# Another order of the expert blocks in a mixture-of-experts step: wide blocks in twos at three places, the fullest expert between two small blocks, two small blocks last

## The reference

```python
logits = x2 @ w_router + b_router             # 536 tokens, 32 experts
top_v, top_i = lax.top_k(logits, 4)
gates = jax.nn.softmax(top_v, axis=-1)
# for each expert e, on the tokens xe that chose it:
gu = xe @ w_gate_up[e] + b_gate_up[e]         # 1024 -> 2048
gate, up = gu[:, :1024], gu[:, 1024:]
gate = jnp.minimum(gate, 7.0)
up = jnp.clip(up, -7.0, 7.0)
h = gate * jax.nn.sigmoid(1.702 * gate) * (up + 1.0)
yb = h @ w_down[e] + b_down[e]                # 1024 -> 1024
# y[token] = sum over its 4 experts of gates * yb
```

## Time and profile before

| | |
|---|---|
| median of 3 runs | 1348.79 us (1348.22 to 1349.29) |
| profiled execution | 1349.23 us |
| its span, first to last instruction | 1347.4 us |
| TensorE busy | 1248.3 us, 93% of the span |
| VectorE busy | 831.6 us, 62% |
| ScalarE busy | 608.9 us, 45% |
| moved by DMA | 457.16 MB, mean 339 GB/s |
| of that on SyncE's queue | 435.28 MB, 78.9% of 16 engines' span |

### The profile page before, as it was taken

One profiled execution on the slowest core, in us unless ns is written; L12 is line 12 of the kernel. 1 busy time (PEld: TensorE's weight loads), 2 busy tenths in 40 slices (PEclk: granted clock), 3 DMA queues, 4 the chain that ended last, 5 costly groups with the idle time before them and its releaser, 6 DMA issues.

```text
span 1347.4 us, 18886 instructions
## 1 busy us (share of the span) xinstructions
PE 1248.3 (93%) x6184; PEld 807.3 (60%) x6185; DVE 831.6 (62%) x1352; ACT 608.9 (45%) x826; POOL 145.8 (11%) x158
## 2 busy tenths in 40 slices
PE   7999999899999999999999999799999999999992
PEld 5888854477574747464656576264747474656550
DVE  3896668699393837464655596182937464655643
ACT  4111342478273545354444574172735354453632
POOL 8100011010001010101101000100010101101000
PEclk9999999989999999999999999999999999999996
DMA  9610176399999999999999984999999999999984
GB/s 322 87 38 1 52 259 287 131 334 411 355 417 412 419 411 419 405 422 405 414 409 400 416 364 180 406 419 406 421 408 421 404 412 397 401 417 388 421 341 139
DMA packets 67333, 457.16 MB, mean 339 GB/s; under 512 B 15916, under 2 KB 19508, under 8 KB 34520
## 3 DMA queue, kind: packets, MB, share of 16 engines
q1 hardware_dynamic: 56344, 435.28, 78.9%
q0 software_dynamic: 10944, 21.30, 6.7%
HBM read 440.26 MB, written 23.50 MB: 344 GB/s over the span
## 4 chain that ended last, share of the span: by engine, by line
PE 42%; DMA 20%; DVE 8%; issue 5%; ACT 4%; DVEq 0%; SPq 0%; ACTq 0%; POOLq 0%; POOL 0%
PE bank L2144 24%; DMA ring_lo<-in_w_gate_up 15%; PE bank L2254 12%; DVE w_lo L2376 6%; DMA ymix<-ffn_in,idx_next 3%; ACT w_hi L1964 3%; PE bank L2265 2%; DMA token_sums<-ymix,row_cur 1%; PE bank L2134 1%; PE bank L2127 1%; DVE cmix L2394 1%; DVE cmix L2397 1%; PE bank L2230 1%; ACT cmix L1983 0%; PE bank L2274 0%
## 5 line engine op out<-in xcount | busy, mean ns | idle before, releaser
L2376 DVE TENSOR_TENSOR w_lo<-ring_lo,w_hi 128x1024 fp32r<-128x1024 f32 x271 | 315.6, 1220 | 101.0 <-ACT w_hi L1964 99.9
L1964 ACT ACTIVATE w_hi<-ring_lo 128x1024 fp32r<-128x1024 f32 x271 | 270.2, 1052 | 86.8 <-DMA ring_lo<-in_w_gate_up 64.4
L2254 PE MATMUL bank<-ring_lo,x_s 128*64 128x512 f32 x960 | 215.9, 597 | 0.4 <-ACT x_s L1973 0.4
L2144 PE MATMUL bank<-w_hi,x_hi 128*128 128x512 f32 x544 | 179.5, 412 | 8.9 <-DVE x_lo L2382 6.7
L2144 PE MATMUL bank<-w_lo,x_hi 128*128 128x512 f32 x544 | 173.8, 402 | 0.0
L2144 PE MATMUL bank<-w_hi,x_lo 128*128 128x512 f32 x544 | 172.2, 398 | 0.0
L2376 DVE TENSOR_TENSOR w_lo<-w_out,w_hi 128x1024 fp32r<-128x1024 f32 x136 | 161.7, 1220 | 6.0 <-ACT w_hi L1964 5.2
L1964 ACT ACTIVATE w_hi<-w_out 128x1024 fp32r<-128x1024 f32 x136 | 140.0, 1053 | 31.8 <-PE bank L2144 31.6
L1892 POOL DMA_INDIRECT token_sums<-ymix,row_cur x33 | 57.2, 1732 | 742.3 <-ACT ymix L1994 705.3
L2254 PEld LDWEIGHTS bank<-ring_lo,x_s 128*64 128x64 f32 x960 | 65.0, 137 | 119.1 <-issue 117.0
L2144 PEld LDWEIGHTS bank<-w_hi,x_hi 128*128 128x128 f32 x544 | 102.4, 196 | 40.1 <-issue 18.8
(11 more groups left out here) (444 smaller groups left out, 1407.4 us busy)
## 6 DMA issues: line engine op xcount, KB each, us to landing
ring_lo<-in_w_gate_up SPq DMA_DIRECT2D x128, 2048.0 KB, 18.8
w_out<-in_w_down SPq DMA_DIRECT2D x128, 1024.0 KB, 20.5
ring_lo<-in_w_in SPq DMA_DIRECT2D x3, 2048.0 KB, 21.1
w_out<-in_w_out SPq DMA_DIRECT2D x2, 2048.0 KB, 8.7
x<-in_x_prompt SPq DMA_DIRECT2D x6, 512.0 KB, 11.3
bias<-bias_rows SPq DMA_DIRECT2D x132, 3.0 KB
ring_lo<-in_w_in SPq DMA_DIRECT2D x2, 1024.0 KB, 9.7
token_sums<-x SPq DMA_DIRECT2D x4, 512.0 KB
```

What stands on the lines that cost most here:

```text
L1964: nc.scalar.activation(high(j), raw(j), ACT.Copy).then_inc(s["w_hi"], 1)
L2144: last = nc.tensor.matmul(bank[b + u][:], v[:, k, :], part(j)[:, u, :], start=(j == 16 and first), stop=(k == KD - 1 and part is high and ...
L2254: last = nc.tensor.matmul(bank[2 * half][64 * u:64 * u + 64, :], x_s[:, k % 4, 64 * (k // 4):64 * (k // 4) + 64], gu[:, k, :, half, 256 * ...
L2376: v.tensor_tensor(low(j), raw(j), high(j).bitcast(F32), ALU.subtract).then_inc(s["w_lo"], 1)
```

## The change

The core of the diff (the same order is written out on ScalarE and VectorE as well; the line numbers of the changed file are other ones):

```diff
@@ -47,12 +47,19 @@
 GATE_MAX = LIMIT / (1.0 + math.exp(-ALPHA * LIMIT))
 S_SLOTS = P // 2
 Q_SLOTS = P // 4
-EARLY, LATE = 7, 7
-TOP = 2 * EARLY + 2
+PAIRS = (3, 3, 3, 3)
+FIRST_EXTRA = 2 + 2 * PAIRS[0]
+TOP = FIRST_EXTRA + 2 + 2 * PAIRS[1]
 REST_OF_TOP = TOP + 1
-FINAL = TOP + 2 * LATE + 2
+SECOND_EXTRA = TOP + 2 + 2 * PAIRS[2]
+FINAL = SECOND_EXTRA + 2 + 2 * PAIRS[3]
 NPOS = FINAL + 1
-SMALL_RANK = EARLY + LATE + 3
+SMALL_RANK = sum(PAIRS) + 5
+RUNS = (2, FIRST_EXTRA + 1, TOP + 2, SECOND_EXTRA + 1)
+SMALLS = (0, PAIRS[0], PAIRS[0] + PAIRS[1] + 2, PAIRS[0] + PAIRS[1] + PAIRS[2] + 2)
+WIDES = (2, PAIRS[0] + 3, PAIRS[0] + PAIRS[1] + 4, PAIRS[0] + PAIRS[1] + PAIRS[2] + 5)
+TOP_WIDE, TOP_SMALL = WIDES[2] - 1, SMALLS[2] - 1
+LAST_SMALL = sum(PAIRS) + 3
...
+            g.iota(pairs[:, 0], pattern=[[1, n]], base=SMALL_RANK + SMALLS[run] - run // 2, channel_multiplier=0)
+            g.iota(pairs[:, 1], pattern=[[1, n]], base=WIDES[run] + 1 - run // 2, channel_multiplier=0)
...
+        def pair_loads(run, i, extra=False):
+            q = RUNS[run] + 2 * i
+            load_behind_small(expert_at(sp, q + 1), q + 1, i + SMALLS[run])
+            load_behind_wide(expert_at(sp, q + 2), q + 2, i + WIDES[run], not extra)
+
+        with sp.Fori(0, PAIRS[0] - 1) as i:
+            pair_loads(0, i)
+        pair_loads(0, PAIRS[0] - 1, True)
+        load_behind_wide(expert_at(sp, FIRST_EXTRA + 1), FIRST_EXTRA + 1, WIDES[1] - 1, True)
+        with sp.Fori(0, PAIRS[1]) as i:
+            pair_loads(1, i)
+        load_behind_small(expert_at(sp, TOP), TOP, TOP_SMALL - 1)
         bias_rows_small(expert_at(sp, REST_OF_TOP), REST_OF_TOP)
-        load_behind_small(expert_at(sp, TOP + 2), TOP + 2, EARLY, True)
-        with sp.Fori(0, LATE) as i:
-            load_behind_small(expert_at(sp, 2 * i + (TOP + 3)), 2 * i + (TOP + 3), i + (EARLY + 1))
-            load_behind_wide(expert_at(sp, 2 * i + (TOP + 4)), 2 * i + (TOP + 4), i + (EARLY + 3), True)
+        load_behind_small(expert_at(sp, TOP + 2), TOP + 2, TOP_SMALL, True)
+        with sp.Fori(0, PAIRS[2] - 1) as i:
+            pair_loads(2, i)
+        pair_loads(2, PAIRS[2] - 1, True)
+        load_behind_wide(expert_at(sp, SECOND_EXTRA + 1), SECOND_EXTRA + 1, WIDES[3] - 1, True)
+        with sp.Fori(0, PAIRS[3]) as i:
+            pair_loads(3, i)
+        load_behind_small(expert_at(sp, FINAL), FINAL, LAST_SMALL - 1, True)
...
+        def pair(run, i, side, extra=False):
+            q = RUNS[run] + 2 * i
+            gather(q + 1)
+            added(q - 1)
+            scatter(q, side, 2)
+            gather(q + 2, 1 if extra else 2)
+            added(q)
+            scatter(q + 1, 1 - side)
+
+        with pool.Fori(0, PAIRS[0] - 1) as i:
+            pair(0, i, 0)
+        pair(0, PAIRS[0] - 1, 0, True)
+        gather(FIRST_EXTRA + 1, 2)
+        added(FIRST_EXTRA - 1)
+        scatter(FIRST_EXTRA, 0)
+        with pool.Fori(0, PAIRS[1]) as i:
+            pair(1, i, 1)
         gather(TOP)
         added(TOP - 2)
-        scatter(TOP - 1, 1)
...
+            pair(3, i, 1)
+        gather(FINAL, 2)
+        added(FINAL - 2)
+        scatter(FINAL - 1, 1, 2)
...
-        def small(q, side, sq, loads, lq=None):
+        def small(q, side, sq, loads, lq=None, next_parts=4):
             for half in range(2):
                 if half == 0:
                     act.wait_ge(t["s_first"], t0["s_first"] + sq + 1)
@@ -2055,10 +2087,13 @@
                 take_x(q + 1)
                 split(loads + 1, lq, 2)
                 split(loads + 1, lq, 3)
+            elif next_parts == 2:
+                take_x_small(q + 1)
             act.wait_ge(t["s_used"], t0["s_used"] + LOADS * sq + LOADS)
             take_y(q, side, [4], [512])
             if lq is None:
-                take_x_quarter(q + 1)
+                if next_parts == 4:
+                    take_x_quarter(q + 1)
...
-                if k == 4 and next_parts == 1:
+                if k == 4 and next_parts < 4:
                     pe.wait_ge(s["idx"], q + 2)
-                    x_transposes(q + 1, 1)
-                    set_bias(q + 1)
+                    x_transposes(q + 1, next_parts)
+                    if next_parts == 1:
+                        set_bias(q + 1)
+                    else:
+                        set_bias_small(q + 1)
                 small_down(k)
...
-        small(FINAL, EARLY + LATE + 1, FINAL, over_expert(pe, 0), 4)
+
+        def pair(run, i, extra=False):
+            q = RUNS[run] + 2 * i
+            small(q, i + SMALLS[run], q + 1 if run < 2 else q, expert_at(pe, q + 1), 1)
+            wide(q + 1, i + WIDES[run], expert_at(pe, q + 2), 1 if extra else 2)
+
+        with pe.Fori(0, PAIRS[0] - 1) as i:
+            pair(0, i)
+        pair(0, PAIRS[0] - 1, True)
+        wide(FIRST_EXTRA, WIDES[1] - 1, expert_at(pe, FIRST_EXTRA + 1), 2)
+        with pe.Fori(0, PAIRS[1]) as i:
+            pair(1, i)
+        small(TOP - 1, TOP_SMALL - 1, TOP, expert_at(pe, TOP), 1)
+        wide_with_rest(TOP, TOP_WIDE, TOP_SMALL, expert_at(pe, REST_OF_TOP), expert_at(pe, TOP + 2))
+        with pe.Fori(0, PAIRS[2] - 1) as i:
+            pair(2, i)
+        pair(2, PAIRS[2] - 1, True)
+        wide(SECOND_EXTRA, WIDES[3] - 1, expert_at(pe, SECOND_EXTRA + 1), 2)
+        with pe.Fori(0, PAIRS[3]) as i:
+            pair(3, i)
+        small(FINAL - 1, LAST_SMALL - 1, FINAL - 1, expert_at(pe, FINAL), 2)
+        small(FINAL, LAST_SMALL, FINAL, over_expert(pe, 0), 4)
         overflow(pe, over)
 
     @block.vector
...
+        def small_to_small(q, side, sq, e_next):
+
+            pick(e_next, zero[:, 0:1], 2)
+            next_slots(q, side, 2, sq + 1)
+            small_swiglu(q, 0)
+            small_swiglu(q, 1)
```

More of the change, by code:

```diff
@@ L1919, in _ @@
         scatter(1, 1)
[L1920 to L1929, removed]
+        def pair(run, i, side, extra=False):
[14 more added lines that the diff above has]
+            pair(1, i, 1)
         gather(TOP)
         added(TOP - 2)
-        scatter(TOP - 1, 1)
+        scatter(TOP - 1, 1, 2)
         gather(REST_OF_TOP, 4)
@@ L1938, in _ @@
         scatter(REST_OF_TOP, 1, 4)
-        with pool.Fori(0, LATE) as i:
-            gather(2 * i + (TOP + 3))
-            added(2 * i + (TOP + 1))
-            scatter(2 * i + (TOP + 2), 0, 2)
-            gather(2 * i + (TOP + 4), 2)
-            added(2 * i + (TOP + 2))
-            scatter(2 * i + (TOP + 3), 1)
+        with pool.Fori(0, PAIRS[2] - 1) as i:
+            pair(2, i, 0)
+        pair(2, PAIRS[2] - 1, 0, True)
+        gather(SECOND_EXTRA + 1, 2)
+        added(SECOND_EXTRA - 1)
+        scatter(SECOND_EXTRA, 0)
+        with pool.Fori(0, PAIRS[3]) as i:
+            pair(3, i, 1)
+        gather(FINAL, 2)
+        added(FINAL - 2)
+        scatter(FINAL - 1, 1, 2)
         added(FINAL - 1)
@@ L2082, in _, with pair @@
         wide(1, 1, 1, 2, 2)
-        with act.Fori(0, EARLY - 1) as i:
-            small(2 * i + 2, 0, i, 2 * i + 3, i + 2)
-            wide(2 * i + 3, 1, i + 2, 2, 2 * i + 4)
-        small(TOP - 2, 0, EARLY - 1, TOP - 1, EARLY + 1)
-        wide(TOP - 1, 1, EARLY + 1, 1, TOP)
-        wide_with_rest(TOP, 0, EARLY + 2, EARLY, TOP + 1)
-        with act.Fori(0, LATE) as i:
-            small(2 * i + (TOP + 2), 0, i + (EARLY + 1), 2 * i + (TOP + 2), i + (EARLY + 3))
-            wide(2 * i + (TOP + 3), 1, i + (EARLY + 3), 2, 2 * i + (TOP + 3))
-        small(FINAL, 0, EARLY + LATE + 1, FINAL)
-        overflow(act, lambda b: quarter(b + NPOS, b + (EARLY + LATE + 2)))
+        def pair(run, i, side, extra=False):
+            q = RUNS[run] + 2 * i
+            loads = q + 1 if run < 2 else q
+            small(q, side, i + SMALLS[run], loads, i + WIDES[run])
+            wide(q + 1, 1 - side, i + WIDES[run], 1 if extra else 2, loads + 1)
+        with act.Fori(0, PAIRS[0] - 1) as i:
+            pair(0, i, 0)
+        pair(0, PAIRS[0] - 1, 0, True)
+        wide(FIRST_EXTRA, 0, WIDES[1] - 1, 2, FIRST_EXTRA + 1)
+        with act.Fori(0, PAIRS[1]) as i:
+            pair(1, i, 1)
+        small(TOP - 1, 1, TOP_SMALL - 1, TOP, TOP_WIDE)
+        wide_with_rest(TOP, 0, TOP_WIDE, TOP_SMALL, TOP + 1)
+        with act.Fori(0, PAIRS[2] - 1) as i:
+            pair(2, i, 0)
+        pair(2, PAIRS[2] - 1, 0, True)
+        wide(SECOND_EXTRA, 0, WIDES[3] - 1, 2, SECOND_EXTRA)
+        with act.Fori(0, PAIRS[3]) as i:
+            pair(3, i, 1)
+        small(FINAL - 1, 1, LAST_SMALL - 1, FINAL - 1, next_parts=2)
+        small(FINAL, 0, LAST_SMALL, FINAL)
+        overflow(act, lambda b: quarter(b + NPOS, b + (LAST_SMALL + 1)))
         def square(q):
```

67 lines of the change are left out of this document (33 added, 34 removed).

## The result

The changed kernel takes 1341.66 us (median of 4 runs, 1340.89 to 1341.85), the kernel before 1349.04 us beside it (4 runs, 1348.22 to 1349.68): a ratio of 0.9947, interval [0.9934, 0.9959]. The prediction said 1341.7. A second comparison gave 1341.09 against 1347.62 us, 0.9952 [0.9939, 0.9966]. The profiled execution took 1341.48 us, with a span of 1339.6 and a mean clock of 0.976.

A forecast was written before the change was run, and what follows sets the result against it. The weight stream was taken to pace the blocks of experts. Gains of 3.1 us (hole) and 4.0 us (end), 7.1 us off the profiled 1349.23, gave 1342.1; allowing for its 0.44 us above the median, 1341.7 us, range 1337 to 1348.5.

The forecast's parts named there:

- in every pair of the first half: Pairs of a small and a wide block: the chain of waits goes through the wide block's fourth weight load.
- The twos of wides cost nothing: Adjacent wide blocks at positions 7/8 and 23/24: costed at nothing, at most 4.4 us each.
- The backlog: Weight loads queued ahead in the steady pairs: about 12 us of other work, hiding the 4.4 us of a second wide block.
- 9 positions of 32.5 us: From position 7's fourth load landing at 508.96 us to position 16's, expected at 801.4 us.
- a sign of being wrong: Behind one of the twos of wides: a DMA share clearly under 1 would show the prediction wrong.
- The hole, 3.1 us: Empty queue at the overflow: its products begin at 822.1 instead of 825.24 us, ending it 3.1 us sooner; bounds 0 and 6.
- The end, 4.0 us: Last small block, behind another small one, is paced by its loads and ends at 1316.0 us: 4.0 us gained, bounds 0 and 6.
- the turn through the other engines: Last small block: 1 us added for the turn through ScalarE and VectorE, which has less to hide behind.
- The lower clock: Last block: TensorE's clock at 1.2 GHz after a wait of some 2 us could cost 1 to 2 us.
- A: Only one of the two gains, at the overflow or the last block, comes: some 1345 us; chance 0.13.
- B: Nothing changes: empty stretch at the overflow and end as long as before, or gains given back; 1348.8 us, chance 0.14.
- C: Late gathers of the second wide blocks at both twos drain the queue: slower, some 1354.5 us; chance 0.11.

The follow-up runs named there:

- the early gather: Changed kernel with the gather of position 19 ahead of the wait for the fullest expert's scatter: 1342.96 us, 0.9965 of the kernel before.
- the first half alone: Kernel before with only the first-half order changed (wides at 7 and 8, fullest expert behind a small block), run twice: ratios 0.9993 and 0.9981 to it.
- each half: Kernel before with only the first-half or only the second-half order changed, each run twice: ratios 0.9993 and 0.9981, then 0.9974 and 0.9973.
- Five wides: Changed kernel with five wide blocks in a row at positions 7 to 11 and four small ones at 12 to 15: 1345.37 us, 0.998 of before.
- the best kernel: Changed kernel with the overflow's products ahead of unit 14 of the fullest expert and the gather of position 19 earlier: 1337.64 and 1337.27 us.

## Why the prediction was right, point by point

**What bounds it.** The stream of weights, and at the overflow TensorE as well. (In the first pair, positions 2 and 3, the chain before had no weight load yet; the prediction's "in every pair of the first half" holds from the second pair on.) To give TensorE time (the early gather, a third small block last) brought nothing; to let the loads go out sooner brought 3.5 us, but only once TensorE could follow. The second condition was not in the prediction, which took an earlier load behind the overflow as a gain by itself; at the 2.5 us of this change it did hold (the first half alone, with the load 2.8 to 3.0 us earlier, kept 2.0 to 2.3 us of it).

**The twos of wides cost nothing.** Nearly. The backlog covers one step of 4.4 us with some 8 to spare: at position 8 the first product follows the last one of position 7 with no gap (536.4 us), and the share is 1.01 in the stretch around it. But the step "9 positions of 32.5 us" from the fourth load of position 7 to that of position 16 came out 1 us long: 800.9 − 507.6 = 293.3 us, and 293.6 in the second profile, against the 292.5 of the sum. From the fourth load of position 23 to that of position 32 it was 1301.92 − 1010.71 = 291.2 us, and 291.0 in the second profile, against 9 × 32.2 = 289.8. Behind the second two the share is a little under 1, which the prediction named as a sign of being wrong; but the kernel before has as low a share behind a single wide block. The changed kernel first, then the kernel before:

```profile
1040.00:1080.00 40.00, 39.51 (x190) 29.14 (x190) 28.70 (x37) 23.81 (x28) 5.38 (x4) 1.00 0.95 378
```

```profile
1080.00:1120.00 40.00, 37.72 (x173) 24.76 (x173) 22.03 (x31) 17.84 (x22) 3.82 (x3) 0.96 0.96 393
```

So where the 1 us and the 1.2 to 1.4 us went, and whether the twos cost them, is not shown.

**The hole, 3.1 us.** Right in its mechanism, 0.6 us too large: 552.9 − 550.45 = 2.45 us. The 20.7 us from the fourth load to the overflow's products were right (821.36 − 800.86 = 20.5); the landing of that load was the part that was off: 800.86 − 273.04 = 527.8 us after the first product, where the sum had 801.4 − 274.4 = 527.0.

**The end, 4.0 us.** The whole of 6.4 to 6.7 us less 2.45 leaves some 4.1. The fourth load of the last block was expected at 1301.9 and landed at 1301.92, though with a start 1.4 us sooner, so 1.4 us late counted from the first product, 0.65 of it from the hole; from that landing to the last product it took 13.5 us against 14.1. The steps of gate and up behind the landing took 1307.91 − 1301.96 = 5.95 us, where the sum had 5.6 and 1 us for the turn through the other engines: the turn costs some 0.35 us. Half of the one miss is made good by the other. The lower clock that the prediction named as a possible 1 to 2 us came in other kernels, and in neither profile of this one.

**The sum.** 7.1 us were forecast, 6.4 to 6.7 measured between first and last product, and 6.5 to 7.4 between medians. That the time came within 0.1 us of the forecast is in part luck: the spread from one execution to the next is larger than that (the runs of before in one comparison go from 1346.0 to 1349.6 us).

**The rivals.** A fell because each half shows its gain by itself, B because both ends of the stream moved. C fell because the gathers ahead of the second wide blocks were on time: they went out at 511.34 and 1014.51 us and landed 10.8 and 11.0 us later, while C needed more than 27 us. The 15 us that the prediction gave such a gather were those of gathers behind a small block. The one of the two that existed before, in GpSimd's timeline, and its landing:

```profile
772.68 1.18 POOL L1884 DMA_INDIRECT ymix<-ffn_in,idx_next  x1 [10.78 <-DVE idx_next L2361]
```

```profile
DMA to landing us min/median/max: 11.2/11.2/11.2
```

It took 11.2 us, so C had some 4 us more against it than was counted. Five wides show when such a backlog is used up: at the fourth step of 4.4 us in a row, not the first.

On these gathers the page DMA: Bandwidth & Descriptors of the Trainium skill, in its section on queues, rings and completion order, says that each DMA engine serves the queue rows with work in turn. The trace agrees in that a gather doesn't wait for the loads queued ahead of it: the one that went out at 511.34 us landed at 522.1, ahead of loads issued at 499.24 and 504.2 us, which took 24.6 and 24.7 us. But its 11 us are still far above the 4.4 us that the prediction estimated from that page's rate, and no run here shows how the packets alternate.

## What to carry to other kernels

When the weight stream sets the pace, the order of the work is worth only what it does to the stretches in which the stream is empty and to what is left after the last load; look for these two and cost everything else by the backlog. A hole ends when the last user of the buffer lets go of it, so it shrinks with whatever that user waits for; but a shorter hole pays only if the compute chain behind it can follow, and two edits that give nothing alone may give 3.5 us together. Compare profiles from the first instruction that the change could reach, not from the start of the program: here that took the difference between two executions of the kernel before from 1.6 us to under 0.1 us, and left 0.3 us at most for the change and its halves. What varies behind that point stays: 4.6 us between the two profiles of the best kernel.

## What the runs showed of the hardware

After waits of equal length TensorE's clock fell in some executions and not in others. Ten of the profiles are of kernels with small blocks in the last two positions; each has a wait for the fourth load in the last block. The clock fell behind it in six (waits of 1.94, 2.02, 2.65, 2.67, 2.77 and 3.01 us) and stayed in four (1.91, 1.92, 2.65 and 2.75 us). TensorE's timeline in the changed kernel, and in the one with the overflow's products alone moved:

```profile
1301.96 4.51 PE L2302 MATMUL bank<-ring_lo,x_s 128*64 128x512 f32 x20 [2.65 <-DMA ring_lo<-in_w_gate_up]
```

```profile
1300.74 6.21 PE L2306 MATMUL bank<-ring_lo,x_s 128*64 128x512 f32 x20 [2.65 <-DMA ring_lo<-in_w_gate_up]
```

Where it fell, 20 matmuls took 6.21 us (once 6.00) in place of 4.51, 1.7 us at a place that no later wait hides. What decides it is not shown.

The start of the experts varied from 272.1 to 274.4 us over the fourteen profiles, though ahead of it the programs' instructions differ in one small table only. And the time from the last product to the end of the span was 24.2 to 25.0 us in all but one of them, and 25.9 where the load of the sums, the next step of the chain, took 5.92 us in place of 4.68.
